# Neighbourhood attention: the values' transposes go to another PSUM buffer and another place in the order

## The reference

```python
s_loc = s_loc + bias[None]                       # window scores with a relative position bias
s_ctx = jnp.einsum('brqhd,bchd->brhqc', ...)     # scores with the context
logits = jnp.concatenate([s_loc..., s_ctx], axis=-1)
p = jax.nn.softmax(logits, axis=-1)
o = (p over the window) @ v + (p over the context) @ vc
y = (o * silu(g)) @ w_out
```

## Time and profile before

| | |
|---|---|
| median of 3 runs | 2746.35 us (2741.91 to 2749.76) |
| the profiled execution: its own time | 2745.68 us |
| the profiled execution: span from first to last instruction | 2743.9 us |
| mean granted TensorE clock | 0.976 |
| TensorE matmuls busy | 94% of the span |
| VectorE busy | 62% |
| ScalarE busy | 35% |
| attention stage | about 318 to 703 us of the span |

### The profile page before, as it was taken

How to read it: one execution, slowest core, us unless ns; L and a number is a source line. 1 busy time by engine, 2 the same in 40 slices (tenths; PEclk the granted TensorE clock), 3 DMA queues, 4 the chain that set the end, 5 groups by cost and what they waited for, 6 DMA issues and landing times. The chain is left out here.

```text
span 2743.9 us, 36258 instructions
## 1 busy us (share of the span) xinstructions
PE 2583.4 (94%) x14006; PEld 2195.8 (80%) x14006; DVE 1698.9 (62%) x2680; ACT 959.6 (35%) x1488; POOL 163.7 (6%) x96
## 2 busy tenths in 40 slices
PE   6999899998899999899899899999998989999999
PEld 3888788887788877778787788888886778888887
DVE  4987766666678988854667864444335456544433
ACT  3222444444333233433462422222223345333222
POOL 0000000000000000000471000000000036000000
PEclk9999999999999999989999999999999999999999
DMA  6243434343355625312003343434111110233332
GB/s 232 91 154 129 141 132 150 131 144 128 115 184 192 192 86 161 115 53 100 1 1 100 111 128 122 134 114 137 62 62 60 62 46 1 62 106 94 92 99 93
DMA packets 88539, 296.30 MB, mean 108 GB/s; under 512 B 10288, under 2 KB 13360, under 8 KB 87856
## 3 DMA queue, kind: packets, MB, share of 16 engines
q1 hardware_dynamic: 88368, 293.98, 32.8%
HBM read 291.85 MB, written 2.10 MB: 107 GB/s over the span
## 5 line engine op out<-in xcount | busy, mean ns | idle before, releaser
L950 PE MATMUL turns<-h_hi,w_hi 128*128 128x512 f32 (+1 forms) x2488 | 800.2, 365 | 36.5 <-DVE h_lo L1535 24.9
L950 PE MATMUL turns<-h_hi,w_lo 128*128 128x512 f32 (+1 forms) x2488 | 779.7, 356 | 0.0
L950 PE MATMUL turns<-h_lo,w_hi 128*128 128x512 f32 (+1 forms) x2488 | 777.7, 356 | 0.0
L950 PEld LDWEIGHTS turns<-h_hi,w_hi 128*128 128x128 f32 x2488 | 427.7, 191 | 125.8 <-DVE h_lo L1535 41.1
L1302 ACT ACTIVATE w_hi<-w_raw 128x1024 fp32r<-128x1024 f32 x300 | 316.0, 1054 | 528.0 <-PE turns L950 517.3
L950 PEld LDWEIGHTS turns<-h_lo,w_hi 128*128 128x128 f32 x2488 | 427.6, 191 | 67.5 <-issue 1.0
L950 PEld LDWEIGHTS turns<-h_hi,w_lo 128*128 128x128 f32 x2488 | 426.8, 191 | 67.7
L1532 DVE TENSOR_TENSOR w_lo<-w_raw,w_hi 128x1024 fp32r<-128x1024 f32 x300 | 366.3, 1221 | 80.4 <-ACT w_hi L1302 80.0
L1535 DVE SCALAR_TENSOR_TENSOR x_lat<-turns,modulation,x_lat 128x512 f32<-128x512 f32 (+1 forms) x121 | 86.0, 711 | 291.8 <-PE turns L950 288.8
L950 PE MATMUL turns<-m_hi,w_lo 128*128 128x512 f32 (+1 forms) x768 | 237.1, 358 | 0.0
L950 PE MATMUL turns<-m_hi,w_hi 128*128 128x512 f32 (+1 forms) x768 | 236.5, 357 | 0.0
(11 more groups left out here) (255 smaller groups left out, 3329.8 us busy)
## 6 DMA issues: line engine op xcount, KB each, us to landing
w_raw<-in_wpack SPq DMA_DIRECT2D x300, 512.0 KB, 3.6
ada_raw<-in_adapack SPq DMA_DIRECT2D x176, 512.0 KB, 4.1
bias<-in_bias SPq DMA_DIRECT2D x64, 320.0 KB, 3.0
ada_first_a<-in_adapack SPq DMA_DIRECT2D x12, 512.0 KB, 8.7
x_lat<-in_xT SPq DMA_DIRECT2D x1, 2048.0 KB, 8.4
x_ctx<-in_ctxT SPq DMA_DIRECT2D x2, 1024.0 KB, 8.7
ada_first_b<-in_adapack SPq DMA_DIRECT2D x4, 512.0 KB, 14.8
cond_rows<-in_crow SPq DMA_DIRECT2D x4, 512.0 KB, 10.4
```

The lines of the kernel that those rows point to most:

```text
L950: ins = pe.matmul(dst[:, lo:lo + sz], w, x[:, lo:lo + sz], start=first and n == 0, stop=last and n == 2)
```

## The change

The step `vtrans` of pairs 1 to 7 is moved from i = 0 (behind `soft(8t)`, ahead of `pv(8t - 2)`) to i = 1: behind `trans(8t + 1)` and ahead of the second half of the gate's projection and of `soft(8t + 1)`, or, in the last pair, of the `early` tiles. It writes columns 0 to 767 of the turn buffer that `pvmm(8t - 2)` used, instead of half 1 of `scores`. TensorE now waits for the end of `pv(8t - 2)` (`s.behind`) instead of `na_rest_made`; that semaphore is removed, and `values_turned` tells ScalarE and VectorE that the transposes are there. The turn buffer is free for the next turn but one when `v_lo` is made. On ScalarE the step stays exempt from the general wait. No instruction with arithmetic is added or removed, and no DMA is moved.

```diff
         if n % 2 == 0 and n:
             mm = na_pv(n - 2)
         na_trans(n)
+        if i == 1 and t:
+            vt = add("vtrans")
+            vt.after, vt.of, vt.behind = [made["v"]], last_mm, pv[n - 3]
+            last_mm.reader = vt
         if i % 2 == 0 and t + 1 < KT:
...
         na_soft(n)
         if i == 6 and t + 1 < KT:
             late_query(cur["q"])
-        if i == 0 and t:
-            vt = add("vtrans")
-            vt.after, vt.behind = [made["v"]], n
         if n % 2 == 0 and n:
             na_pv_out(n - 2, mm)
+            last_mm = mm
...
                     if s.behind is None:
                         free_scores(1, s)
+                        dst = SP_[:, 1, :]
                     else:
-                        pe.wait_ge(na_rest_made, s.behind + 1)
-                        last_scores[1] = s
+                        wait_steps([s.behind])
+                        dst = PS[:, s.turn % 2, :]
                     for n in range(NT):
-                        ins = pe.transpose(SP_[:, 1, n * P:n * P + P], T3[:, n * P:n * P + P], IDN[:])
-                    ins.then_inc(score_mm[1], 1)
+                        ins = pe.transpose(dst[:, n * P:n * P + P], T3[:, n * P:n * P + P], IDN[:])
+                    ins.then_inc(score_mm[1] if s.behind is None else values_turned, 1)
...
                 elif s.kind == "vtrans":
-                    scores_in(1, s)
-                    give(act.activation(Vh[:], SP_[:, 1, 0:TT].rearrange("p (n f) -> p n f", f=P), ACT.Copy))
+                    if s.of is None:
+                        scores_in(1, s)
+                    else:
+                        act.wait_ge(values_turned, nth_values[s])
+                    src = (SP_[:, 1, :] if s.of is None else ps)[:, 0:TT].rearrange("p (n f) -> p n f", f=P)
+                    give(act.activation(Vh[:], src, ACT.Copy))
...
                 elif s.kind == "vtrans":
-                    scores_in(1, s)
+                    if s.of is None:
+                        scores_in(1, s)
+                    else:
+                        dve.wait_ge(values_turned, nth_values[s])
                     take()
-                    done(rest(Vl[:], SP_[:, 1, 0:TT].rearrange("p (n f) -> p n f", f=P), Vh[:]))
+                    src = (SP_[:, 1, :] if s.of is None else ps)[:, 0:TT].rearrange("p (n f) -> p n f", f=P)
+                    done(rest(Vl[:], src, Vh[:]))
...
-                        if s.na and x is not None:
-                            ins.then_inc(na_rest_made, 1)
```

More of the change, by code:

```diff
@@ L611, in plan @@
     for s in steps:
-        n = {"final": 1, "hnorm": 0, "back": 0, "nstat": 1, "adacol": 1, "rope": 1, "vtrans": 1, "scores": s.st, "trans": 1 if s.na else None}.get(s.kind)
+        n = {"final": 1, "hnorm": 0, "back": 0, "nstat": 1, "adacol": 1, "rope": 1, "vtrans": 1 if s.of is None else None, "scores": s.st, "trans": 1 if s.na else None}.get(s.kind)
         if n is not None:
@@ L737, in build_blocks @@
         tile_scaled = sem("tile_scaled")
-        na_scores_read, na_rest_made = sem("na_scores_read"), sem("na_probability_rests")
+        na_scores_read, values_turned = sem("na_scores_read"), sem("na_values_turned")
         ctx2_in, dft_in, sp_in, out_done = sem("ctx2_in"), sem("dft_in"), sem("sp_in"), sem("out_done")
@@ L752, in build_blocks @@
         nth_tile = {s: n + 1 for n, s in enumerate(by_kind["ntile"])}
+        nth_values = {s: n + 1 for n, s in enumerate(s for s in by_kind["vtrans"] if s.of is not None)}
         na_scores = [s for s in by_kind["scores"] if s.na]
```

## The result

The changed kernel takes 2754.57 us (median of 13 runs, 2750.54 to 2761.88) against 2744.92 us for the kernel before beside it (13 runs, 2738.86 to 2749.76). The ratio is 1.0036 with a 95% interval of 1.0027 to 1.0045: **slower by 0.36%**, about 9.9 us. The profiled execution is the one of 2754.57 us; its mean granted clock is 0.976, as before.

A forecast was written before the change was run, and what follows sets the result against it. The prediction took each pair change to end, for TensorE, with `soft(b)` on VectorE. Seven changes at 1.20 us gave 8.4, less 0.1 for rounding, so +8.3 on 2746.35: 2754.7 us, range 2749 to 2760.

The forecast's parts named there:

- TensorE up to `trans(b)`: At a pair change, `trans(b)` no longer waits for `v_lo` and starts at S + 0.14, 1.73 us earlier.
- S: End of the scaling that ends `soft(a)` at a pair change; 374.73 us in the kernel before.
- What is late next: Value transposes wait for `o_lo`, ending at S + 1.50; TensorE idles about 1.0 us, starting them at S + 1.64.
- What TensorE waits for at the end: Sign: value product L1222 waits for the scaling about 1 us in each middle pair.
- The chain behind them: From value transposes through `v_hi` to `v_lo`: 0.89 + 0.94 + 0.96, so `v_lo` ends at S + 4.43, uncovered.
- The difference: Ahead of `soft(b)`, `v_lo` at S + 4.43 replaces `o_lo` at S + 3.23; `soft(b)` ends 1.20 us later.
- the bounds of 0.95 and 1.34: Per-change loss: 0.95 us if transposes to `v_hi` take less, 1.34 if TensorE pays another 0.14 wake-up.
- Neither engine finds slack: From `pvmm(a)` on, TensorE and VectorE are both late by the same 1.20 us, so neither recovers it.
- The sum against the clock: Seven changes sum to +8.3 us; a lower clock in the last pair would lose 1.7 us or twice that.
- the rival with 0.20: Last pair's holes lower the clock, losing 1.7 us or twice that: 2756.4 to 2758.1 us; chance 0.20.
- The faster rival: `trans(b)` 1.73 us earlier ends `soft(b)` earlier if `v_lo` ends before S + 3.23: 2737.8 us; chance 0.07.
- Mostly made up: Later work in middle pairs uses 0.49 us idle TensorE time each, returning 3.4 us: 2751.3 us; chance 0.13.

The follow-up runs named there:

- e6: Changed kernel, but the first four of six value transposes (columns 0 to 511) don't wait for the end of `pv(a-2)`; ratio 1.0017, middle pair 49.45 us.
- e3: Changed kernel with `vtrans` at i = 0 right behind `pv(a-2)`, ahead of `scores(b+1)` and `trans(b)` on TensorE; ratio 1.0061, middle pair 51.3 to 51.5 us.
- e4: Kernel before, old buffer kept, with `vtrans` moved behind `na_pv_out` in the list; ratio 1.0052, middle pair 51.3 us.
- e10: e3 plus five plain matmuls of ones (2.15 us) before TensorE's wait for `o_lo` at each change; ratio 1.0022, middle pair 49.90 us.
- e9: e3 plus ten plain matmuls of ones (4.3 us) before TensorE's wait for `o_lo` at each change; ratio 1.0067, middle pair 51.16 us.

## Why the prediction was right

The predicted 2754.7 us was measured at 2754.57, and slower was the likelier side. That the two agree to 0.13 us is luck. The prediction added 8.3 to 2746.35, the median of three runs; thirteen runs of the kernel before give 2744.92, 1.43 lower, and the difference of the medians is 9.65. What holds is the mechanism and the size of its term. Step by step:

- *TensorE up to `trans(b)`*: start at S + 0.15 (0.14 predicted), the wait for `v_lo` gone.
- *What is late next*: `o_lo` at S + 1.50, exactly as put; transposes at S + 1.65 (1.64); TensorE's wait there 0.76 in the row (about 1.0 in the step of the prediction, which counted the end of `trans(b)` from issue to issue and not with the way through the array, and 0.75 where it priced the clock).
- *What TensorE waits for at the end*: the value product waits 0.76 us for the scaling, where the signs said about 1. The prediction's chain left out one wait that stands between: `scores(b + 2)` waits 0.34 for the reduce, which is late too. It takes nothing more, since `soft(b)` still ends last.
- *The chain behind them*: `v_lo` ends at S + 4.50 against 4.43. The term that was short is the one that no row showed: from the first transpose to `v_hi` it is 379.29 - 378.35 = 0.94, not 0.89; the rest is rounding in the gaps behind it.
- *The difference*: 1.24 to 1.26 us a change against 1.20, so 8.7 us against 8.3. It lies inside the bounds of 0.95 and 1.34.
- *Neither engine finds slack*: all middle pairs keep the full 1.24.
- *The sum against the clock*: the rival with 0.20 did occur, in one of two profiles of the changed kernel, with 2.0 us where 1.7 was put. At one in two it would add 1.0 on average, but two profiles can't fix that share, and the ratio's interval, 7.4 to 12.4 us, can't tell 8.7 from 9.7.

*The faster rival* fell by the row that it named: `v_lo` ended at S + 4.50, far behind S + 3.23. The Trainium skill, "Perfetto Trace Analysis", section "Optimization Strategy", says to look for the gaps of the engine being optimised and to make what ends them start sooner. By that rule, taken no further than the gap ahead of `trans(b)`, the sum would be minus 8.5 us; the trace disagrees, with 1.24 us more at each change. Taken one step further, it leads to `soft(b)`, which ends the gap ahead of the value product. *Mostly made up* fell too: no pair gave anything back.

What I did not see was how cheap the cure is. The prediction states that the step stands ahead of `soft(b)` in the list and that nothing covers its chain; one place further down, the same chain runs beside `soft(b)` and the loss of 1.24 becomes a gain of 0.34 in a middle pair.

## What to carry to other kernels

When a wait of the busiest engine is to be removed, follow the work that was waiting to its consumer, and ask what that consumer's engine does in the meantime: `trans(b)` came 1.7 us earlier and its reader was still queued behind another engine's chain. In a hand-written order in which all engines walk one list, put a step whose result is needed late behind the step whose result is needed soon, and look whether a wait for a buffer's last reader has to hold for the whole buffer (in e6 it was dropped for columns 0 to 511, which gave 0.49 us a pair). Price a stall by its length in one piece as well as by its sum: in e3 and e4 one hole of 2.95 or 2.45 us was followed by the lower clock in nearly every pair, and four holes with a sum of 2.4 us were not.

## What the hardware showed that was not expected

- One hole of 2.95 us a pair in TensorE's work (e3), or one of 2.45 (e4), was followed by a stretch at half clock that cost about 1.5 us, in every pair of e3 and from the second pair on in e4; the changed kernel's four waits, which sum to 2.4 us from just ahead of S to the value product, left the clock at 1.00. So did the first hole of e4, 2.44 us long. With 2.2 us of filler in the hole of e3 (e10) it stayed at 1.00 too.
- A matmul of 256 columns with ones, whose operands are plain fp32 and not fp32r as the scores' are, took (432.20 - 427.89) / 10 = 0.43 us in e9's filler, against 0.12 from start to start for the 256-column matmuls of the scores in the stretch of the earlier trace rows.
- The copy of the values, the same instruction with the same shape, started 0.94 us behind the first transpose from the turn buffer and 0.89 from the scores' buffer, where the scores' matmuls and not the gate's followed the transposes. It is not what follows: in e3's first change the scores' matmuls follow the transposes from the turn buffer, and it is 0.94 again (377.00 to 377.94). Whether the buffer itself or the way ScalarE waits for it makes the 0.05 us is open.
